# Top-4-of-32 expert block: gate and up biases of the wide rounds added by VectorE from repeated rows in place of four TensorE matmuls

## The reference

```python
logits = xf @ w_router + b_router
top_v, top_i = lax.top_k(logits, TOP_K)          # 4 of 32 experts
gates = jax.nn.softmax(top_v, axis=-1)
...
def expert_block(args):                          # one block of rows of one expert
    e, toks, wts = args
    xb = xf[toks]
    gt = jnp.minimum(xb @ w_e_gate[e] + b_e_gate[e], SWIGLU_LIMIT)
    up = jnp.clip(xb @ w_e_up[e] + b_e_up[e], -SWIGLU_LIMIT, SWIGLU_LIMIT)
    act = (up + 1.0) * (gt * jax.nn.sigmoid(gt * SWIGLU_ALPHA))
    return (act @ w_e_down[e] + b_e_down[e]) * wts[:, None]
...
out = h + scatter_add(rows)                      # then a last rmsnorm
```

## Time and profile before

| | us |
|---|---|
| median of 3 executions | 2727.32 |
| lowest, highest | 2718.69, 2734.62 |
| the profiled execution | 2717.3 |
| its span (first to last instruction) | 2715.7 |
| mean granted TensorE clock | 0.971 |
| busy: PE, DVE, ACT, POOL | 2555.9, 1736.5, 1283.5, 511.5 |

### The profile page before, as it was taken

The page is one execution under the profiler, slowest core; times in us unless marked ns, Lnnn a source line. Parts: engine busy times, 40 slices in busy tenths (PEclk is TensorE's granted clock), DMA queues, the critical chain, the costliest instruction groups (busy, mean ns, idle before and its releaser), DMA issues.

```text
span 2715.7 us, 61354 instructions
## 1 busy us (share of the span) xinstructions
PE 2555.9 (94%) x24101; PEld 2154.9 (79%) x24101; DVE 1736.5 (64%) x2053; ACT 1283.5 (47%) x1402; POOL 511.5 (19%) x593
## 2 busy tenths in 40 slices
PE   7898889898998999898999999999999999999995
PEld 5676767675998999788888888788878888888884
DVE  8657566564222112354677677676779999999996
ACT  3313131321221111242665666665667777777776
POOL 6000000000000000123433433433421111111111
PEclk9999989997999999998999999999999999999997
DMA  5000000000112112345777877877889999999999
GB/s 126 16 3 23 5 18 10 18 10 2 39 40 61 43 27 70 121 78 131 284 280 275 297 279 271 295 282 269 298 327 390 381 379 379 377 383 386 379 379 341
DMA packets 143110, 527.82 MB, mean 194 GB/s; under 512 B 18411, under 2 KB 72271, under 8 KB 91010
## 3 DMA queue, kind: packets, MB, share of 16 engines
q1 hardware_dynamic: 120642, 480.00, 47.4%
q0 software_dynamic: 22336, 45.93, 6.9%
HBM read 492.01 MB, written 33.86 MB: 194 GB/s over the span
## 4 chain that ended last, share of the span: by engine, by line
PE 86%; DVE 4%; DMA 3%; issue 3%; ACT 3%; POOL 0%; SPq 0%; ACTq 0%; DVEq 0%; POOLq 0%
PE bank L949 33%; PE bank L2215 13%; PE bank L2216 13%; PE bank L2217 13%; PE bank L2224 5%; DMA raw_first<-in_w_e_up 1%; PE bank L2187 1%; PE bank L2110 1%; DVE xmix L713 1%; PE bank L2256 1%; PE bank L2111 1%; PE bank L2112 1%; PE bank L2203 1%; PE bank L2162 1%; PE bank L2288 1%
## 5 line engine op out<-in xcount | busy, mean ns | idle before, releaser
L2018 DVE TENSOR_TENSOR w_lo<-raw_first,w_hi 128x2048 fp32r<-128x2048 f32 x267 | 601.9, 2287 | 107.7 <-ACT w_hi L1790 107.4
L1790 ACT ACTIVATE w_hi<-raw_first 128x2048 fp32r<-128x2048 f32 x268 | 515.9, 1925 | 227.3 <-DMA raw_first<-in_w_e_up 88.3
L2215 PE MATMUL bank<-w_hi,x_hi 128*128 128x512 f32 x1056 | 421.7, 399 | 4.2 <-ACT yo_rows L1842 4.2
L2217 PE MATMUL bank<-w_hi,x_lo 128*128 128x512 f32 x1056 | 413.2, 391 | 0.0
L2216 PE MATMUL bank<-w_lo,x_hi 128*128 128x512 f32 x1056 | 412.8, 391 | 0.0
L2018 DVE TENSOR_TENSOR w_lo<-raw_rest,w_hi 128x2048 fp32r<-128x2048 f32 x132 | 298.9, 2285 | 0.2
L1790 ACT ACTIVATE w_hi<-raw_rest 128x2048 fp32r<-128x2048 f32 x132 | 252.5, 1918 | 97.4 <-DMA raw_rest<-in_w_e_down 43.5
L949 PE MATMUL bank<-xm_hi,ring_hi 128*128 128x256 f32 (+1 forms) x896 | 260.3, 291 | 18.8 <-DVE dz L910 8.1
L949 PE MATMUL bank<-xnT,ring 128*128 128x260 f32 x880 | 246.8, 425 | 13.9 <-ACT pb L545 9.9
L949 PE MATMUL bank<-xm_hi,ring_lo 128*128 128x256 f32 (+1 forms) x896 | 254.1, 284 | 0.0
L949 PE MATMUL bank<-xm_lo,ring_hi 128*128 128x256 f32 (+1 forms) x896 | 253.0, 282 | 0.0
(11 more groups left out here) (380 smaller groups left out, 4150.3 us busy)
## 6 DMA issues: line engine op xcount, KB each, us to landing
raw_first<-in_w_e_up SPq DMA_DIRECT2D x134, 1024.0 KB, 7.1
raw_first<-in_w_e_gate SPq DMA_DIRECT2D x68, 1024.0 KB, 7.0
raw_rest<-in_w_e_gate SPq DMA_DIRECT2D x68, 1024.0 KB, 5.4
raw_first<-in_w_e_down SPq DMA_DIRECT2D x66, 1024.0 KB, 7.0
raw_rest<-in_w_e_down SPq DMA_DIRECT2D x66, 1024.0 KB, 8.5
ring<-in_w_in SPq DMA_DIRECT2D x40, 512.0 KB, 3.9
h_all<-in_x SPq DMA_DIRECT2D x8, 512.0 KB, 15.1
hn_d<-hn SPq DMA_DIRECT2D x8, 512.0 KB, 7.2
```

The source lines that it names most:

```text
L1790: nc.scalar.activation(w_hi[:, j % NRING, :, :], raw_piece(j), ACT.Copy).then_inc(hi_done, 1)
L2018: nc.vector.tensor_tensor(w_lo[:, j % NRING, :, :], raw_piece(j), w_hi[:, j % NRING, :, :].bitcast(f32), ALU.subtract).then_inc(lo_done, 1)
L2215: nc.tensor.matmul(ps[:, :], hi, w_hi[:, slot, k, :], start=start and k == 0, stop=False)
L2217: ins = nc.tensor.matmul(ps[:, :], lo, w_hi[:, slot, k, :], start=False, stop=stop and k == HK - 1)
```

## The change

In wide rounds the main tile's gate and up biases no longer go through TensorE. POOL loads two more tiles, the gate row and the up row of the expert, each repeated on all 128 partitions (`bias_all`, 2 x 512 KB, in SBUF that held other things before the experts start). DVE adds them while it reads PSUM, into `g_t` or `u_t`, signals itself, and clips from there to the same place. The last product of pieces 1, 3, 5 and 7 now closes the group. TensorE's wait for the biases moves to piece 8, where the down bias is used. Counts of `bias_got` go from 80 to 112 per wide round. Plain rounds keep the old form.

```diff
+    bias_all = Plan(nc, shared['start'] + 4 * NT * D)("bias_all", [128, 2, D])
...
+    main_biased = sem("main_biased")
...
                 for c in range(4):
                     pool.dma_start(bias_ov[OV * c:OV * (c + 1), :, :, :].rearrange("p g h f -> p (g h f)"),
                                    bias_parts[bass.ds(e, 1), c, :].to_broadcast([OV, 4 * 128])).then_inc(bias_got, 16)
+                for x, rows in enumerate((b_gate, b_up)):
+                    pool.dma_start(bias_all[:, x, :], rows[bass.ds(e, 1), :].to_broadcast([128, D])).then_inc(bias_got, 16)
...
                             if t == 1:
                                 dve.wait_ge(ov_used, r * NPIECE + j + 1)
-                                dve.wait_ge(bias_got, r * 80 + 80)
                                 nc.vector.tensor_tensor(g, gp, bias_ov[:, 0, h, :], ALU.add).then_inc(ov_biased, 1)
                                 dve.wait_ge(ov_biased, r * 4 + 2 * h + 1)
+                                gp = g
+                            if t == 0 and wide:
+                                dve.wait_ge(bias_got, r * 112 + 112)
+                                nc.vector.tensor_tensor(g, gp, bias_all[:, 0, HC * h:HC * (h + 1)], ALU.add).then_inc(main_biased, 1)
+                                dve.wait_ge(main_biased, r * 4 + 2 * h + 1)
                                 gp = g
                             nc.vector.tensor_scalar(g, gp, LIMIT, None, ALU.min).then_inc(gu_read[t], 1)
...
                             dve.wait_ge(aT_ps[t], r * 2 + h + 1)
+                            if t == 0 and wide:
+                                nc.vector.tensor_tensor(u, up, bias_all[:, 1, HC * h:HC * (h + 1)], ALU.add).then_inc(main_biased, 1)
+                                dve.wait_ge(main_biased, r * 4 + 2 * h + 2)
+                                up = u
...
-                    ins = products(ps, x_hi, x_lo, j % NRING, HK * (j % 2), j % 2 == 0, False)
-                    if j == 1:
-                        pe.wait_ge(bias_got, r * 80 + 80 if wide else r * 16 + n_wide * 64 + 80)
-                    if j % 2 == 1:
+                    ins = products(ps, x_hi, x_lo, j % NRING, HK * (j % 2), j % 2 == 0, wide and j % 2 == 1)
+                    if j == 1 and not wide:
+                        pe.wait_ge(bias_got, r * 16 + n_wide * 96 + 112)
+                    if j % 2 == 1 and not wide:
                         ins = nc.tensor.matmul(ps[:, :], kind_row[:, g % 2, :], bias_t[:, HC * h:HC * (h + 1)],
                                                start=False, stop=True)
...
+                    if j == 8 and wide:
+                        pe.wait_ge(bias_got, r * 112 + 112)
```

More of the change, by code:

```diff
@@ L1393, in experts_program @@
     bias_ov = Plan(nc, ex.at)("bias_ov", [128, 2, 2, 128])
+    bias_all = Plan(nc, shared['start'] + 4 * NT * D)("bias_all", [128, 2, D])
+    assert shared['start'] + 4 * NT * D + 4 * 2 * D <= raw_at
     fin_junk = ex("fin_junk", [128, D])
@@ L1716, in on_gpsimd @@
                                                      in_=yo_rows[:, n, :], in_offset=None, compute_op=ALU.add).then_inc(y_out[1], 16)
-        pool.wait_ge(bias_got, rounds * 16 + n_wide * 64 + 80)
+        pool.wait_ge(bias_got, rounds * 16 + n_wide * 96 + 112)
         pool.wait_ge(rows_in[0], rounds * 16 + 32)
```

## The result

| | before | after |
|---|---|---|
| median of 4 executions, us | 2730.77 | 2758.72 |
| lowest, highest | 2718.69, 2734.62 | 2750.32, 2767.13 |
| the profiled execution | 2717.3 | 2756.05 |
| wide round, mean of 12 in the trace | 50.27 | 52.74 |
| from the start of the second wide round to the end | 1373.5 | 1412.4 |

The change is slower: ratio 1.012, 95% interval 1.0079 to 1.016. The first part, up to the second wide round, varies by 10 us and more between executions of one kernel and has nothing to do with the change, so the traces are compared from there on: 38.9 us more, 31.2 in the 13 wide rounds and 7.7 in the plain ones.

The account below looks back on a forecast made before the run. Wide rounds were taken as bound by TensorE, a weight-load chain 0.3 us behind. Removing 12.8 us of matmuls and adding 8.3 us of waits gave -4.5 us from 2727.3, so 2723 us, range 2709 to 2741.

Parts of the forecast that it names:

- TensorE is the bound, with a second chain 0.3 us behind, at L2209: Wide rounds: TensorE busy 50.00 of 50 us; the weight load behind `a_lo`, awaited before piece 6, has 0.3 us mean slack.
- 12.8 us off TensorE's stream: Wide rounds: 56 bias matmuls removed at 0.228 us each, 0.91 us per round.
- DVE: nothing: Wide rounds: four adds and clips from SBUF, 2.7 us more per round, fit in DVE's 14.5 us free and cost nothing.
- The bias tiles land in time, but for 1 or 2 us in the first round: DVE at piece 1: tiles there at about 1496.4, wanted at about 1498; late landing, chance 0.02.
- POOL's queue: `next_t` 1.6 us later, and with it gathers and scatters: Two issues of 0.79 us delay the index load, gathers and scatters by 1.6 us; POOL itself costs nothing.
- The hole takes 1.9 us of the 2.9: DMA engines, idle from 1492: absorbs 1.9 us of the added 1 MB's 2.9; 1.0 us pushes later loads.
- The sum: Whole kernel: -12.8 us of matmuls plus 8.3 us of waits at L2209 gives -4.5 us.
- d = 0.5: Delay of piece 7's landing against TensorE, in us per wide round; taken as 0.5, with ends -2.8 and +2.9.
- The sign named for d: Interval from the load of pieces 6 and 7 to the second `w_hi`, 10.1 us before, was to tell piece 7's delay.
- The price per round: At L2209 each of 13 rounds waits 0.46 us plus piece 7's delay, less its slack; 8.3 us in all.
- The second rival: At L2209: the weight load becomes the round's bound, +13.8 us (2741) to +26.8 us (2754); chance 0.13.
- The rival on the clock: TensorE's granted clock falls with the waits, 10 us or more slower; chance 0.01.

Follow-up runs that it names:

- e1: The change with the bias rows loaded only in the first round, so later wide rounds add the first expert's; ratio 0.9952 to the kernel before.
- e3: The kernel before without the four bias matmuls of a wide round, no loads or adds in their place; ratio 0.9991 to the kernel before.
- e2: The kernel before with the two bias loads added per wide round and not used, bias matmuls kept; ratio 1.0155 to the kernel before.
- e6: The change with SP issuing the two bias loads behind the loads of the next round's pieces 2 and 3; ratio 1.0089 to the kernel before.
- e7: The change with only the gate row loaded anew each wide round, half a megabyte; ratio 1.0111 to the kernel before.
- e5: e3 with three POOL memsets delaying gathers and scatters, no byte added; ratio 1.0068 to the kernel before.
- e13: e8 once more, with more executions; ratio 0.999 (0.9963 to 1.0017) to the kernel before.
- e10: The change unedited, measured again beside the kernel before; 2759.93 us, ratio 1.0141.
- e11: The change with POOL holding a wide round's scatters until piece 7 of the next round is rounded; ratio 1.0168 to the kernel before.
- e4: The change with POOL issuing the two bias loads 14 us earlier, after the round's last add; ratio 0.999 to the kernel before.
- e8: The change with SP issuing the two bias loads early, behind the loads of the next round's pieces 0 and 1; ratio 0.999 to the kernel before.
- e12: e4 with POOL holding a wide round's scatters until piece 7 of the next round is rounded; ratio 1.0152 to the kernel before.

## Why the prediction was wrong

It gave 2723 us and a range up to 2741; 2758.7 came. Beside the kernel before, measured again at 2730.8, that is a loss of 28 us where a gain of 4.5 was forecast. By its own steps:

- **TensorE is the bound, with a second chain 0.3 us behind, at L2209.** Right as to the chain and its place. But L2222 holds only 16.2 us of waits; the larger part, 21.2 us, was lost ahead of it.
- **12.8 us off TensorE's stream.** Right in size, as far as one trace tells. In e1, 13 rounds are 0.51 us shorter (6.6 us), and waits of 3.4 - 1.0 and 1.9 us more overflow make it 10.9 of 13 x 0.91 = 11.9.
- **DVE: nothing.** Nothing shows against it, by e1 and e3. The add takes 0.69 us as its row said, the clip from SBUF 0.43, within the ends 0 and 0.7. Timeline of DVE at piece 1 of the first round:

```profile
1301.72 0.69 DVE L2062 TENSOR_TENSOR g_t<-bank,bias_all 128x512 f32<-128x512 f32 x1 [4.99 <-DMA bias_all<-in_b_e_up]
1302.45 0.43 DVE L2065 TENSOR_SCALAR g_t<-g_t 128x512 f32<-128x512 f32 x1
```

- **The bias tiles land in time, but for 1 or 2 us in the first round.** Right: the 4.99 us above is the only such wait of DVE, and TensorE lost 0.7 + 1.3 us to it. Issues took 0.56 us, not 0.79, and landings 6.9 us on the median, not 7.1.
- **POOL's queue: `next_t` 1.6 us later, and with it gathers and scatters.** Too small. The issue is 1.2 us later, but the load of indices now stands behind a megabyte and lands 6.4 us after its issue (median) where it took 4.5. I costed two issues and forgot the transfers that they put ahead of a tiny one that is waited for. The gather is 3.1 us later.
- **The hole takes 1.9 us of the 2.9.** Right.
- **The sum: TensorE's stream only gets shorter, and all that a late megabyte does is the wait at L2209.** The step that failed most. The 64 overflow products behind piece 1 took 45.7 us in 13 rounds in place of 24.5, 21.2 us of a stall (last section) that no term of the sum holds. e2 shows that the loads make it (44.1 with the old matmuls in place), e1 that nothing else of the change does (26.4). The stall also holds back the loads of pieces 6 and 7, which wait for these products; the sum took their release as fixed.
- **d = 0.5, "since the later scatter speaks for less".** Also too small, and with the wrong sign in its reason. d was defined against TensorE. Counted from the end of the overflow products, piece 7 was 0.6 us later than before in the ten stalled rounds and 3.0 in the three others, 1.1 on the mean; where no stall comes it is 2.0 (e6) and 2.3 (e7). In ten rounds d was near the forecast by luck: the loads started late and then took 9.9 us in place of 10.5. The reason fails in e5, where late gathers and scatters cost piece 7 1.3 us and take nothing off. The sign named for d, the time from the load to the second `w_hi`, could not have told it: its mean is 10.5 us before and after, since it misses a load that goes out late.
- **The price per round.** Right when d is measured in this way. 13 x (0.46 + d) - 4.1 gives, with what came behind it, 16.7 and 16.2 us of waits for the change (d = 1.14), 27.5 and 27.6 for e6 (1.97), 32.0 and 32.0 for e7 (2.32), 7.6 and 7.9 for e13 (0.44), and 21.8 and 24.1 for e5 (1.53). (At d = 0.5 and 1 it gives 8.4 and 14.9, where the prediction has 8.3 and 14.8.)

The balance of the 13 rounds: -11.9 for the matmuls, +15.2 waits for `a_lo`, +21.2 for the overflow behind piece 1, +6.4 for the clock (both below), together 30.9 of 31.2. In e10 the same sum is -11.9 + 13.1 + 19.8 + 1.6 = 22.6 of 22.1. In the plain rounds, 7.7 us (3.3 in e10), only one wait is named, 3.2 us of L2269 for `bias_t` in the first: the last wide round also fetches bias tiles, for a plain round that does not use them. The rest of the 7.7 is open.

The second rival (the weight load becomes the bound, 0.13) had the right place, and its size for the median, 13.8 us and more, fits the 28 that came. As a mechanism it holds for three rounds of the change and for e5 to e7: there the loads take 12.0 to 12.8 us, and its sentence on the scatter, that it "may fall right on the loads of pieces 6 and 7 and leave an idle stretch where it was", describes e5. It got a small chance since I asked for "nearly the whole megabyte outside the hole", and e5 has such a delay with no byte at all. In the other ten rounds most of the loss is the stall, which no rival had. Two signs of being wrong came true: TensorE "waits somewhere else for long", and plain rounds changed "by more than a few us in total". The rival on the clock (0.01) came true in part: four waits of 1.8 to 3.9 us did what one of 1.3 us had not.

## What to carry to other kernels

A bulk load that runs ahead of a small, awaited one delays all that waits for the small one by more than its issue: the gather was 3.1 us late where 1.6 were counted, and still 1.9 with the bulk in another queue (e6). When data comes late, look first at when its load was issued and what released it, and only then at what slowed it on the way. Where the DMA engines are full, ask of each transfer between which two others it falls, and move it by an experiment that adds no byte (a delay on the issuer) before counting megabytes. With a second chain 0.3 us behind the bound, a saving of 0.9 us per round was worth about half (0.39 in e3, 0.51 in e1), and a delay beyond those 0.3 us counts in full.

## What was not expected of the hardware

**The clock fell after waits of about 2 us and more.** The prediction argued from one wait of 1.3 us that left the clock at 1.00. After the change, four waits (2.08 us before 1471.84, 3.92 before 1578.62, 2.94 before 1684.45, 1.77 before 1739.14) were followed by a fall. Stretches around the first:

```profile
1471.00:1473.00 2.00, 1.16 (x5) 0.97 (x6) 1.93 (x6) 1.49 (x2) 0.46 (x3) 1.00 0.85 287
1473.00:1476.00 3.00, 3.00 (x10) 2.33 (x9) 3.00 (x3) 1.75 (x4) 0.00 (x0) 0.55 1.03 431
1476.00:1480.00 4.00, 4.00 (x38) 3.06 (x40) 2.08 (x2) 2.47 (x2) 0.00 (x0) 0.91 0.14 57
```

and TensorE's timeline there:

```profile
1471.84 0.30 PE L2222 MATMUL bank<-ident,u_ov 128*128 128x128 f32 x1 [2.08 <-DVE a_lo L2035]
...
1474.16 0.63 PE L2229 MATMUL bank<-w_lo,x_hi 128*128 128x512 f32 x1
1474.58 0.63 PE L2230 MATMUL bank<-w_hi,x_lo 128*128 128x512 f32 x1
```

Starts are 0.42 to 0.43 us apart instead of 0.23 (the lower level, 1.2 GHz), and the products of pieces 6 and 7 take 7.3 us instead of 5.7: each such wait costs 1.6 us more than itself, 6.4 in all. It is no rule: the wait of 2.55 us in e5's round at 1549.80 was followed by 5.7 us, and so were one of 2.78 in e10 and one of 3.17 in e6.

**TensorE stalled with no wait that the profile shows.** The 64 small matmuls behind piece 1 took 1.95 us; in ten of the 13 rounds after the change they take 3.6 to 4.2:

```profile
1505.24 2.03 PE L2237 MATMUL bank<-raw_first,x_ov 128*32 128x128 f32 x50
1507.56 0.45 PE L2237 MATMUL bank<-raw_first,x_ov 128*32 128x128 f32 x5 [0.28 <-issue]
1508.33 0.42 PE L2237 MATMUL bank<-raw_first,x_ov 128*32 128x128 f32 x4 [0.33 <-issue]
1509.05 0.43 PE L2237 MATMUL bank<-raw_first,x_ov 128*32 128x128 f32 x5 [0.30 <-issue]
```

After 50 of them the rest come in bursts of 4 or 5 every 0.7 to 0.8 us. It is in every kernel where POOL has a whole megabyte in front of the gather (the change, e2, e10, and less in e11), faintly in e1, e3 and e4 (2.0 to 2.1 us a round on the mean), never with the loads in SP's queue or halved (e6, e7, e8, e13), nor in e5 and e12. It is the largest term of the loss in the change, but it is hardly a loss on top of the rest: where it is missing, the loads of pieces 6 and 7 take longer and the waits for `a_lo` take its place (e7: 32.0 us and the same round of 52.74, with 13.7 us of clock). That the instructions come late in such bursts is a guess; what TensorE stands still for was not tried and stays open. So does whether it happens in executions that are not profiled; those of the change are as long as the profiled one (2750 to 2767 and 2756 us).
